# Chunkwise mLSTM by pairs of heads, in place of the masked quadratic form over the whole sequence

## What is computed

```python
def step(state, inp):
    c_mat, n_vec, m = state
    b_cum = cumsum(fc)
    logd = where(tril, b_cum[t] - b_cum[s] + ic[s], NEG)
    inter = b_cum + m
    m_t = maximum(inter, max(logd))
    sc = (qc @ kc.T) * exp(logd - m_t)
    w_inter = exp(inter - m_t)
    num = sc @ vc + w_inter * (qc @ c_mat)
    den = sum(sc) + w_inter * (qc @ n_vec)
    h_t = num / maximum(abs(den), exp(-m_t))
    return _mlstm_update(state, kc, vc, ic, fc), h_t
```

## Time and profile before

| | us |
|---|---|
| median of 3 runs | 2063.19 |
| lowest, highest | 2059.76, 2066.58 |
| the profiled execution | 2068.53 |
| its span from first to last instruction | 2066.6 |

### The profile page before, as it was taken

How to read it: one execution, slowest core, us unless ns; L and a number is a source line. 1 busy time by engine, 2 the same in 40 slices (tenths; PEclk the granted TensorE clock), 3 DMA queues, 4 the chain that set the end, 5 groups by cost and what they waited for, 6 DMA issues and landing times.

```text
span 2066.6 us, 25293 instructions
## 1 busy us (share of the span) xinstructions
PE 1933.5 (94%) x10168; PEld 1522.8 (74%) x10168; DVE 634.6 (31%) x1221; ACT 623.6 (30%) x850; POOL 616.3 (30%) x360
## 2 busy tenths in 40 slices
PE   4999989998978999999999969999998969999997
PEld 2888756676857888888888837775666748888885
DVE  2134165454353111111101256202566351111114
ACT  1522223443334321122111244324342353222123
POOL 0442201000434333222222453431010454434343
PEclk8999999999988999999999979996777989999998
DMA  7421134001343222122211162220002343323321
GB/s 272 112 62 52 52 102 140 24 1 38 96 143 111 61 61 81 41 65 67 72 53 54 56 196 61 62 78 25 1 0 76 88 141 100 105 82 109 89 79 49
DMA packets 210361, 163.12 MB, mean 79 GB/s; under 512 B 17669, under 2 KB 190949, under 8 KB 210277
## 3 DMA queue, kind: packets, MB, share of 16 engines
q1 hardware_dynamic: 207744, 157.77, 25.4%
q10 hardware_dynamic: 2532, 4.18, 0.6%
HBM read 159.83 MB, written 2.10 MB: 78 GB/s over the span
## 4 chain that ended last, share of the span: by engine, by line
PE 84%; DVE 7%; ACT 3%; issue 2%; DMA 2%; POOL 1%; ACTq 0%; DVEq 0%; SPq 0%
PE ps L585 56%; PE ps L998 4%; PE ps L983 3%; PE ps L573 2%; PE ps L575 2%; PE ps L574 2%; PE ps L789 2%; PE ps L741 2%; PE ps L766 2%; PE ps L682 1%; DMA ring<-in_mod_w 1%; PE ps L698 1%; DVE xT L1617 1%; DVE xT L1627 1%; PE ps L776 1%
## 5 line engine op out<-in xcount | busy, mean ns | idle before, releaser
L1872 POOL TENSOR_TENSOR wlo<-ring,whi 128x1024 fp32r<-128x1024 f32 (+1 forms) x136 | 317.1, 2344 | 576.5 <-ACT whi L1227 576.3
L585 PE MATMUL ps<-hlo,whi 128*128 128x512 f32 (+1 forms) x1152 | 348.8, 357 | 0.0
L585 PE MATMUL ps<-hhi,whi 128*128 128x512 f32 (+1 forms) x1056 | 324.3, 361 | 10.4 <-DVE modc L1412 8.3
L585 PE MATMUL ps<-hhi,wlo 128*128 128x512 f32 (+1 forms) x1056 | 319.4, 357 | 0.0
L585 PEld LDWEIGHTS ps<-hlo,whi 128*128 128x128 f32 x1152 | 192.5, 190 | 34.6
L585 PEld LDWEIGHTS ps<-hhi,whi 128*128 128x128 f32 x1056 | 175.3, 190 | 39.7 <-DVE modc L1412 8.3
L585 PEld LDWEIGHTS ps<-hhi,wlo 128*128 128x128 f32 x1056 | 173.8, 189 | 30.5
L1675 DVE TENSOR_TENSOR hu<-sg,ps 128x768 f32<-128x768 f32 (+1 forms) x44 | 36.1, 821 | 510.4 <-ACT sg L1239 510.4
L1227 ACT ACTIVATE whi<-ring 128x1024 fp32r<-128x1024 f32 (+1 forms) x136 | 135.0, 1024 | 177.6 <-PE ps L585 176.1
L585 PE MATMUL ps<-uhi,whi 128*128 128x512 f32 (+1 forms) x528 | 160.8, 359 | 0.0
L1590 DVE SCALAR_TENSOR_TENSOR xT<-ps,modc,xT 128x512 f32<-128x512 f32 x96 | 60.6, 659 | 325.0 <-PE ps L585 217.4
(11 more groups left out here) (255 smaller groups left out, 2868.6 us busy)
## 6 DMA issues: line engine op xcount, KB each, us to landing
ring<-in_mod_w SPq DMA_DIRECT2D x96, 512.0 KB, 5.0
ring<-in_ffn_w_in SPq DMA_DIRECT2D x88, 512.0 KB, 3.8
ring<-in_ffn_w_out SPq DMA_DIRECT2D x32, 512.0 KB, 3.6
ring<-in_m_w_in SPq DMA_DIRECT2D x24, 512.0 KB, 3.7
ring<-in_ab_w_in SPq DMA_DIRECT2D x21, 512.0 KB, 4.0
ring<-in_ffn_w_out SPq DMA_DIRECT2D x16, 384.0 KB, 3.2
ring<-in_ab_w_out SPq DMA_DIRECT2D x8, 512.0 KB, 5.1
ring<-in_m_w_out SPq DMA_DIRECT2D x8, 512.0 KB, 5.7
```

Source lines behind the costliest of these rows:

```text
L585: mm = pe.matmul(dst[:, a:b], w, h[:, a:b], start=st, stop=sp_)
L1872: pool.tensor_tensor(wlo[:, s, 0:width], ring[:, (NB[f"ffn{l}"] + s) % RING, 0:width], whi[:, s, 0:width].bitcast(F32), ALU.subtract).then ...
```

## The change

The scan is done by tiles of 128 tokens: inside a tile a masked 128x128 score block, between tiles a state of 64x129 (64 keys by 128 values and one column for the denominator). Two heads are worked together, the one on rows 0 to 63 and the other on rows 64 to 127 of the array or of the output. For each of 4 pairs:

- `key_rows`: 6 transposes turn the pair's keys into token order; VectorE weighs them for both directions (`m_keys`, two operations of 128x768).
- `max_rows` (twice) and `query_rows`: broadcasts of gate rows, now of 40 rows and `fp32r` (a high part on rows 0 to 7, a low part on rows 32 to 39). VectorE scales the queries (`m_queries`).
- 16 exponents of 128 columns on ScalarE; 4 triangles of 128x512 on GpSimd; 8 score matmuls of 128 columns; 4 products of 128x512 on VectorE (`m_weigh`).
- `m_updates`: 20 matmuls of 129 columns, 64 outputs each; `m_states`: 8 VectorE operations of 129 columns that carry the state from tile to tile.
- `m_values`, for each of 4 query tiles: 4 matmuls of 64 rows (query by state) and 4 of 128 rows (score by value), 129 columns. `m_denominators` and `m_stats` on VectorE, for both heads at once.
- The normalisation of pairs 0 to 2 moves to GpSimd; that of the last stays on VectorE.

Ahead of the stage, VectorE and ScalarE make three more sets of gate rows (`wr`, `qr`, the splits `qx` and `nx`) and a rounded copy of the selectors (`selx`). ScalarE's part stands between the floor's exponent and `split_high` of unit 10. The transposes of the gate rows, now 28, stand between units 11 and 12. `mod14` comes wholly behind the last values.

```diff
         act.wait_ge(floor_in, 1)
         act.activation(gbc[0:H_M, :, 0:LAT], gbc[0:H_M, :, 0:LAT], ACT.Exp, scale=-1.0).then_inc(floor_ok, 1)
+        act.wait_ge(wr_in, 1)
+        act.activation(wr[0:H_M, 0, 0:LAT - P], wr[0:H_M, 0, 0:LAT - P], ACT.Exp)
+        act.activation(wr[0:H_M, 1, P:LAT], wr[0:H_M, 1, P:LAT], ACT.Exp)
+        act.activation(wr[0:H_M, :, LAT:T], wr[0:H_M, :, LAT:T], ACT.Exp).then_inc(wr_exp, 1)
+        act.wait_ge(qr_in, 1)
+        step(act.activation(qr[0:H_M, :, :], qr[0:H_M, :, :], ACT.Exp))
+        act.wait_ge(row_zero, 2)
+        act.activation(qx[0:H_M, :, :], qr[0:H_M, :, :], ACT.Copy).then_inc(qx_hi, 1)
+        act.wait_ge(rows_ok, 1)
+        act.activation(nx[0:H_M, :, :], negm[0:H_M, :, :], ACT.Copy).then_inc(nx_hi, 1)
+        act.activation(selx[0:NROW, 0:SEL_W // (T - LAT), LAT:T], selr[0:NROW, :].rearrange("p (k n) -> p k n", n=T - LAT),
+                       ACT.Copy).then_inc(sel_ok, 1)
...
+        def m_scores(p):
+            pe.wait_ge(mexp, 4 * p + 4)
+            for c in range(LT):
+                for b in range(2):
+                    rows, cols = slice(M_DK * b, M_DK * (b + 1)), slice(c * P, (c + 1) * P)
+                    mm = pe.matmul(half(b)[:, cols], mk[rows, p, cols], mq[rows, p, cols], start=True, stop=True)
+            mm.then_inc(m_s, 1)
...
+                        for b in range(2):
+                            rows = slice(M_DK * b, M_DK * (b + 1))
+                            mm = pe.matmul(bank[rows, at:at + M_DV + 1], kw[:, p % 2, d, j, rows], mv[:, j, 2 * p + b, :],
+                                           start=(j == js[0]), stop=(j == js[-1]))
+            mm.then_inc(m_u, 1)
...
+            for d in range(2):
+                n = order_tile(d, c)
+                for b in range(2):
+                    rows = slice(M_DK * b, M_DK * (b + 1))
+                    pe.matmul(dst(b, d), qs[rows, p % 2, d, cols], stt_[rows, p % 2, d, n, :], start=(d == 0), stop=False,
+                              skip_group_check=True)
+            for d in range(2):
+                for b in range(2):
+                    mm = pe.matmul(dst(b, d), pe_[:, p % 2, b, d, cols], mv[:, c, 2 * p + b, :], start=False, stop=True,
+                                   skip_group_check=True)
+            mm.then_inc(m_o, 1)
...
+        for p in range(1, NP + 1):
+            i = LT * (p - 1)
+            if p < NP:
+                key_rows(p)
+                max_rows(p, 0)
+            m_values(i)
+            if p < NP:
+                query_rows(p)
+                max_rows(p, 1)
+            m_values(i + 1)
+            if p < NP:
+                m_scores(p)
+            m_values(i + 2)
+            if p < NP:
+                m_updates(p)
+            m_values(i + 3)
+        mod_rows(1, 4, PS[0])
+        mod_columns(1, 4, PS[0])
...
+        m_exps(0, 0)
+        m_exps(0, 1)
+        for p in range(1, NP + 1):
+            i = LT * (p - 1)
+            if p < NP:
+                m_exps(p, 0)
+            if p >= 2:
+                m_inverse_std(p - 2)
+            if p < NP:
+                m_exps(p, 1)
+        m_inverse_std(NP - 1)
...
+        for p in range(1, NP + 1):
+            i = LT * (p - 1)
+            if p < NP:
+                m_keys(p)
+            m_denominators(i)
+            if p >= 2:
+                step(m_stats(i - 1))
+                m_aggregate(p - 2)
+            if p < NP:
+                m_queries(p)
+            m_denominators(i + 1)
+            m_stats(i)
+            if p < NP:
+                m_weigh(p)
+            m_denominators(i + 2)
+            m_stats(i + 1)
+            if p < NP:
+                m_states(p)
+            m_denominators(i + 3)
+            m_stats(i + 2)
+        step(m_stats(LT * NP - 1))
+        m_aggregate(NP - 1)
```

More of the change, by code:

```diff
@@ L967, in _, with key_rows, max_rows @@
-        mm.then_inc(tr_mm, 1)
-        def m_scores(h):
-            if h == 0:
+        def key_rows(p):
+            if p:
+                pe.wait_ge(m_st, p)
+            else:
                 pe.wait_ge(vg_ev, 10)
                 pe.wait_ge(silu_ev, 8)
-            else:
-                pe.wait_ge(mexp, 12 * h)
+            for t in range(TT):
+                mm = pe.transpose(PS[1][:, t * P:(t + 1) * P], mk[:, p, t * P:(t + 1) * P], ident)
+            mm.then_inc(m_kt, 1)
+        def max_rows(p, b):
+            if b:
+                pe.wait_ge(mexp, 4 * p + 2)
+            elif p:
+                pe.wait_ge(m_st, p)
+            else:
+                pe.wait_ge(vg_ev, 9)
+                pe.wait_ge(sel_ok, 1)
+                pe.wait_ge(nx_lo, 1)
@@ L986, in m_values @@
[L986 to L995, removed]
-                    for j in js:
[L997 to L1000, removed]
@@ L1002, in _, with query_rows @@
-        m_scores(0)
[L1003 to L1007, removed]
-        m_values(H_M - 1)
-        mod_rows(1, 4, PS[2], 2, KD)
-        mod_columns(1, 4, PS[2])
+                mm = pe.matmul(half(d), sel_head(2 * p + b), nx[0:NROW, d, :], start=True, stop=True)
+            mm.then_inc(m_mb, 1)
+        def query_rows(p):
+            pe.wait_ge(m_kw, p + 1)
+            if p == 0:
+                pe.wait_ge(qx_lo, 1)
+            for d in range(2):
+                mm = pe.matmul(half(2 + d), sel_pair(p), qx[0:NROW, d, :], start=True, stop=True)
+            mm.then_inc(m_qb, 1)
@@ new lines, in m_stats, with m_aggregate @@
+        def m_stats(i):
+            p, c = divmod(i, LT)
+            dve.wait_ge(m_num, i + 1)
+            for h in (2 * p, 2 * p + 1):
+                ins = dve.bn_stats(mst[:, h * LT + c, :], hb[:, c, h * M_DV:(h + 1) * M_DV])
+            return ins
+        def m_aggregate(p):
+            for j in range(2 * p * LT, (2 * p + 2) * LT):
+                ins = dve.bn_aggr(mmv[:, j, :], mst[:, j, :])
+            ins.then_inc(mvar, 1)
+        m_keys(0)
+        m_queries(0)
+        m_weigh(0)
@@ L1934, in _ @@
+        m_select(0, 0)
+        m_select(0, 1)
+        for p in range(1, NP + 1):
+            i = LT * (p - 1)
+            if p < NP:
+                m_select(p, 0)
+            if p < NP:
+                m_select(p, 1)
+            if p >= 2:
+                m_normalise(p - 2)
         out_projection(1, wsp_out1)
```

346 lines of the change are left out of this document (217 added, 129 removed).

## The result

The changed kernel takes 1986.18 us, median of 4 runs (1980.92 to 1991.78), against 2064.89 for the kernel before, run beside it (2059.76 to 2070.20). The ratio is 0.9619, with a 95% interval of 0.9582 to 0.9656: 79 us are gained, where 55 were forecast. Its profiled execution took 1980.92, the span in it 1979.2, at a mean granted clock of 0.958.

The account below looks back on a forecast made before the run. TensorE, with work for 94% of the span, was taken as the bound. Pairs, tail and shape changes summed to 123.8 us behind a 6.0 us later start, a gain of 55 and 2008 us; range 1984 to 2034 (8 in 10).

Parts of the forecast that it names:

- rival 2: Stage: clock stays full after the first pair, or 64-row matmuls overlap; pairs 21.6 us, gain 73, 1990 us; chance 0.21.
- front (G to K0): First gate row to first key transposes: ScalarE's new block delays unit 10, TensorE waits 3.8 us; +6.0 us together.
- pair 0: First head pair of the stage: nothing to hide under and half clock; 23.2 us.
- pair 1: Second head pair: no aggregate and no inverse ahead of it; 24 us.
- pair 2: Third head pair, steady state: chain through VectorE, ScalarE and TensorE of 24.0 or 26.0 us, taken as 25.
- tail, to the end of the copy: Behind the last states: four values, normalisation, `mod14` with its loads, copy of its rows; 23 us.
- shape changes, put on top: Changes of TensorE's array shape in the stage: 0.1 us each, 9 a pair, 3.6 us in all.
- I take none: Scores and state part of the values: neighbouring 64-row matmuls do not overlap; eight scores 1.8 us full clock, 3.5 half.
- The prediction's rule that matmuls of 64 rows let the clock fall: TensorE's clock: matmuls using 64 array rows let it fall to half, matmuls of 128 rows raise it.
- Rival 1: Stage: clock never rises; 134.8 us, gain 44, 2019 us, or 2036 without update overlap; chance 0.33 including the VectorE-bound case.
- Rival 3: Stage: each array shape change empties the array, 1.5 us each; slower than before, 2070 us; chance 0.04.
- Rival 4: Stage: VectorE bounds throughout, some 19 us a pair, 2023 us at most; chance 0.33 shared with the clock-never-rises case.

Follow-up runs that it names:

- experiment 1: Changed kernel with score matmuls and the state part of the values ordered head by head, not alternating row halves; K0 to O 114.98 us against 108.17.
- experiment 3: Changed kernel with `m_values` ordered direction by direction, 32 more array shape changes, same matmuls; K0 to O 116.25 us against 108.17.
- experiment 5: Changed kernel with ScalarE's `split_high` of unit 10 moved ahead of its new gate-row block; G to K0 164.3 us against 171.7, K0 to O 111.07 against 108.17.
- experiment 10: Changed kernel run once more, unchanged; 1989.29 us against 2061.81 for the kernel before, ratio 0.9661.
- experiment 6: Changed kernel with ScalarE's inverse deviation moved behind the exponents of both heads; pair 2 17.58 us against 20.01, K0 to O 105.68 against 108.17.
- experiment 9: Changed kernel with unit 10's split and the inverse both moved, forward direction's numerators left out; pair 2 15.66 us, K0 to O 99.03 against 108.17.
- experiment 2: Changed kernel with the update matmuls ordered head by head, so neighbours use the same column half; K0 to O 119.37 us against 108.17.
- after: The changed kernel itself, as first profiled; 1986.18 us, ratio 0.9619 to the kernel before.

## Why the prediction was right, and where it was off

The direction and the mechanism held. The range (1984 to 2034) held by only 2 us, for 1986 came; that is less than the spread of the four executions (1981 to 1992), one of which lies below the range, so that it held at all is in part luck. The forecast was 22 us too high, and the result fell into rival 2, by a mix of both its conditions. The terms:

| term | forecast | measured |
|---|---|---|
| front (G to K0) | +6.0 | +8.4 |
| pair 0 | 23.2 | 21.6 |
| pair 1 | 24 | 17.5 |
| pair 2 | 25 | 20.0 |
| pair 3 | 25 | 19.8 |
| tail, to the end of the copy | 23 | 20.6 |
| shape changes, put on top | 3.6 | in the terms |
| copy to `out1` | 8.2 | 8.7 |

The stage from K0 to the copy is 99.5 in place of 123.8. 24.3 less, 2.4 and 0.5 more in front and behind, make the 21.4 between a gain of 55 and one of 76.5.

**The mis-sized step is "I take none".** For neighbours of 64 rows the prediction named both bounds and took the one without overlap, because each needs loads of its own; experiment 1 shows 1.5 times. Eight scores take 2.08 at half clock and 1.16 at full, not 3.6 and 1.8; in the chain of a steady pair that is some 1.8 of the 5 us. Experiment 1 puts the overlap at 6.8 us in the whole stage. The rule of the Trainium skill that the prediction cited (TensorEngine Tiling, section Theoretical Speedup: up to 2x for a dimension of 64 or less) was nearer the truth than the step that set it aside. Here the gain is 1.5 times for 64 rows, and 1.5 to 1.7 for 64 columns.

**The clock.** The prediction had the front of each pair at full, the scores at half, and the updates at 3.3, between both clocks. They ran at full (2.4) in pairs 1 to 3: 0.9 a pair. In pair 1 there was hardly a gap ahead of the scores (0.73), since VectorE had no old divisors, no aggregate and no inverse ahead of it: the scores began 8.0 behind K1, while they began 10.6 behind K3, and ran at full. The prediction took 1 us off for that. Pair 1 is the term that was furthest off, 24 against 17.5; some of these 6.5 us are the overlap above.

The prediction's rule that matmuls of 64 rows let the clock fall, read off, is neither confirmed nor refuted: the 64-row scores of pair 1 kept it at 1.00 (1444 to 1446), those of pairs 2 and 3 ran into half behind an idle stretch, and in experiment 3 it stayed at half through 12 us without a gap.

**The rest of a steady pair** is small change in one direction: VectorE's front 6.7 (7.3), inverse and exponents 3.9 (4.4), `values(i+2)` no longer behind the product (0.1 in place of 0.9), states 2.45 (2.8), product 2.49 (2.6). Bounds taken from rows of other shapes came out high each time.

**Shape changes.** Taken as 0.1 each on top of the prices; experiment 3 shows 0.2 at full clock and 0.3 at half. The sum had 3.6 for them and, as an estimate from 36 changes at 0.25, would have needed some 9. That didn't show in the total, because the prices for the matmuls were too high. That "the neighbouring matmul records leave no gap there" was a weak argument: ends of matmuls are modelled, and the cost shows in where the next starts. The Trainium skill, TensorEngine Tiling, section Key Properties, has a change of mode drain TensorE; experiment 3 agrees that a change costs something, 0.2 to 0.3 us, and can't show how.

**The front.** The wait ahead of unit 10 was there, released by GpSimd's low part as forecast, and was 5.30 in place of 3.8. Of 2.2 us of slack nothing was left, as forecast; ScalarE's block took 5.7 us (1300.84 to 1306.55) against 6.0. What the step missed is that VectorE came late: the floor's exponent, behind the last convolution, started 57.2 us after G (1299.88), and 55.1 before (1307.23). A convolution on the way, with what GpSimd did beside it, and then the same operation of the last one:

```profile
1282.50 4.57 DVE L1831 TENSOR_SCALAR cacc<-cpad,vcol 128x770 f32<-128x770 f32 x1
...
1284.81 0.95 POOL L2113 MEMSET qx<- 40x1024 f32 x1
...
1285.70 0.95 POOL L2114 MEMSET nx<- 40x1024 f32 x1
```

```profile
1294.68 0.61 DVE L1831 TENSOR_SCALAR cacc<-cpad,vcol 128x770 f32<-128x770 f32 x1
```

The first of them in the kernel before, 39.8 us behind G as here:

```profile
1291.89 2.79 DVE L1718 TENSOR_SCALAR cacc<-cpad,vcol 128x770 f32<-128x770 f32 x1
```

The same operation takes 0.61 with nothing beside it, 2.78 beside a `split_low`, and 4.57 beside a `split_low` and the two memsets that the change adds on GpSimd: 1.8 more. Each time it ended 0.4 us behind the last of these GpSimd operations, in experiments 5 and 10 too. The list of what is moved and added had left out these two. And behind the wait the clock stayed at half for 4 us, which the sum had at nothing (experiment 5: 2 us). Against that the 28 transposes took 1.8 in place of 2.7.

**The tail** is 20.6 in place of 23, and at its end two things come nearly together. The chain goes through the last loads of `mod14` (7.32 us at 1503.62) and TensorE's work on them to 1512.0; VectorE's own last normalisation and product end at 1511.84, and it waits 0.26 us before it copies the rows. So at this end less work for VectorE alone could hardly have gained more.

**The rivals.** Rival 1 (clock never up) falls: 0.90 and 0.91 in pairs 1 to 3. Rival 3 falls with experiment 3. Rival 4 was priced as too weak to hold a pair above 25, and that was right; but pairs got shorter than it reckoned with, and VectorE, at 16.6 us of 20.0, is near enough to be the next bound (experiments 6 and 9). Rival 2 named the pair at 21.6, and 1.6 less came.

**What stays open.** What sets the two paces of the first feed-forward, and where within a pair the clock falls when the stage starts at another time, which moved the stage by up to 3 us with no edit in it. That the memsets lengthened VectorE's operation rests on the timelines of kernels with and without them (4.57 and 2.79); the changed kernel was not run without them.

## What to carry to other kernels

If two small matmuls in a row use different halves of the array, in rows or in columns, count them at two thirds of their time together, and alternate them in the instruction order; then count 0.2 to 0.3 us for every change of shape, so that alternating shapes is what to avoid. When a stream bound by TensorE is cut by half, write out the chain through all engines for each turn of the loop, the first ones too: their missing work is worth as much as a steady turn's overlap. Before a block of small operations is put into an engine's stream, look for a step behind it that feeds TensorE and can go first: a wait there cost its length and another 2 us of half clock.

## What the runs showed of the hardware that was not expected

- The same 3139 matmuls of the first feed-forward took some 547 or some 557 us over the profiles here, and the kernel before had both 557.27 and 546.95: it hangs on the execution. (The 542 us of some expectations is the faster pace as well: in experiments 2 and 5 the chain's row leaves out the first 12 matmuls, and from the first one it is 546.2.) A single profile's span is therefore no measure of a change of 10 us; marks behind that stage are.
- TensorE's clock can be full to the end of an idle stretch and fall once TensorE works again (1.00 in 1481 to 1483, 0.72 in 1484 to 1486, 0.50 in 1486 to 1488), or fall within the stretch (0.80 in 1412 to 1414; in experiment 2 0.60 in 1466 to 1468). Which matmuls paid changed with what came before: the scores of pair 1 took 1.16 us in after and 2.08 in experiment 5, which differs only ahead of the stage.
- A VectorE `tensor_scalar` on SBUF of 0.61 us took 2.79 beside GpSimd's subtraction, and 4.57 where two memsets of 40 x 1024 followed that subtraction. In the tail VectorE's eight normalisations took 3.10 us beside GpSimd's product, where eight took 2.14 before.
